# Eight plain scatter tables in place of one accumulating table, with 112 slots an expert

## The reference, cut to what matters

```python
scores = sigmoid(x @ w_router)                 # 512 tokens x 64 experts
top_idx = the 8 best of scores + bias, from the 4 best of 8 groups
w = scores[top_idx] / sum * 2.5
for expert e, for each of its tokens t:        # 4096 assignments in all
    g, u = split(x[t] @ w_exp_gu[e])           # 1024 -> 2 x 256
    routed[t] += w[t, e] * ((silu(g) * u) @ w_exp_down[e])   # 256 -> 1024
out = layer_norm(2**0.25 * x + routed + shared_expert(x))
```

## Time and profile before

| what | value |
|---|---|
| median of 3 runs | 3268.33 us (3266.63 to 3270.45) |
| the profiled execution | 3269.64 us, its span 3267.9 us |
| granted TensorE clock, mean | 0.938 |
| TensorE matmul busy | 2857.8 us (87%) |
| VectorE busy | 2117.2 us (65%) |
| ScalarE busy | 1468.9 us (45%) |
| POOL busy | 191.9 us (6%) |
| DMA, both queues | 437.13 MB, 32.4% and 8.2% of 16 engines |

### The profile page before, as it was taken

The page is one execution under the profiler, slowest core; times in us unless marked ns, Lnnn a source line. Parts: engine busy times, 40 slices in busy tenths (PEclk is TensorE's granted clock), DMA queues, the critical chain, the costliest instruction groups (busy, mean ns, idle before and its releaser), DMA issues.

```text
span 3267.9 us, 36369 instructions
## 1 busy us (share of the span) xinstructions
PE 2857.8 (87%) x12231; PEld 2118.2 (65%) x12231; DVE 2117.2 (65%) x3326; ACT 1468.9 (45%) x2215; POOL 191.9 (6%) x168
## 2 busy tenths in 40 slices
PE   8899899999989899999988888879776988988883
PEld 6777677887768578877663333655345877777772
DVE  4787546775298577753457885431326988888884
ACT  5666432223255432232224453331224877777772
POOL 0000000000000000000000000000001222222220
PEclk9999999999999899999998888989887999999996
DMA  3222223222311032233220000212018999999995
GB/s 105 59 64 63 79 78 103 86 94 71 104 61 61 26 98 82 77 89 85 83 77 23 0 1 26 78 64 78 30 69 292 356 361 361 361 361 361 361 361 160
DMA packets 292139, 437.13 MB, mean 134 GB/s; under 512 B 27371, under 2 KB 172195, under 8 KB 292035
## 3 DMA queue, kind: packets, MB, share of 16 engines
q1 hardware_dynamic: 272163, 363.42, 32.4%
q0 software_dynamic: 19872, 72.36, 8.2%
HBM read 394.84 MB, written 40.89 MB: 133 GB/s over the span
## 4 chain that ended last, share of the span: by engine, by line
PE 60%; SPq 18%; DVE 11%; ACT 4%; DMA 3%; issue 3%; DVEq 0%; POOLq 0%; ACTq 0%; PEldq 0%
PE tp L1001 36%; SPq L773 12%; SPq L780 5%; PE tp L960 5%; PE tp L1316 1%; PE tp L1054 1%; PE tp L1056 1%; PE tp L1055 1%; DMA uT<-in_w_exp_gu 1%; DMA ytab<-arena 1%; PE mp L1020 1%; PE mp L1034 1%; PE tp L1306 1%; DVE wring_r L2163 1%; PE mp L1231 1%
## 5 line engine op out<-in xcount | busy, mean ns | idle before, releaser
L1001 PE MATMUL tp<-sq_r,arena_r 128*128 128x512 f32 x1152 | 464.4, 403 | 43.2 <-DVE uT_r L2176 25.7
L1001 PE MATMUL tp<-sq_r,wring_r 128*128 128x512 f32 x1152 | 460.1, 399 | 0.0
L1001 PE MATMUL tp<-uT_r,arena_r 128*128 128x512 f32 x1152 | 457.7, 397 | 0.0
L1001 PEld LDWEIGHTS tp<-sq_r,arena_r 128*128 128x128 f32 x1152 | 218.7, 190 | 102.9 <-issue 48.4
L1001 PEld LDWEIGHTS tp<-uT_r,arena_r 128*128 128x128 f32 x1152 | 219.3, 190 | 54.6 <-issue 1.9
L1001 PEld LDWEIGHTS tp<-sq_r,wring_r 128*128 128x128 f32 x1152 | 218.8, 190 | 53.4
L1001 PE MATMUL tp<-arena_r,wring_r 128*128 128x512 f32 x608 | 242.5, 399 | 0.0
L2163 DVE TENSOR_TENSOR wring_r<-wring,arena_r 128x2048 fp32r<-128x2048 f32 x80 | 179.7, 2287 | 79.0 <-ACT arena_r L1581 79.0
L1581 ACT ACTIVATE arena_r<-wring 128x2048 fp32r<-128x2048 f32 x80 | 148.5, 1904 | 56.0 <-DMA wring<-in_w_in 21.5
L1001 PE MATMUL tp<-arena_r,sq_r 128*128 128x512 f32 x480 | 154.6, 404 | 19.6 <-DVE arena_r L2176 19.6
L1800 ACT ACTIVATE arena<-arena 128x512 f32<-128x512 f32 x44 | 27.9, 634 | 292.7 <-DVE arena L2244 292.6
(11 more groups left out here) (446 smaller groups left out, 6267.1 us busy)
## 6 DMA issues: line engine op xcount, KB each, us to landing
arena<-in_w_exp_down SPq DMA_DIRECT2D x64, 1024.0 KB, 18.2
wring<-in_w_exp_gu SPq DMA_DIRECT2D x64, 768.0 KB
uT<-in_w_exp_gu SPq DMA_DIRECT2D x32, 768.0 KB
sq<-in_w_exp_gu SPq DMA_DIRECT2D x32, 768.0 KB
wring<-in_f_up_w SPq DMA_DIRECT2D x22, 1024.0 KB, 5.2
wring<-in_f_up_w SPq DMA_DIRECT2D x44, 512.0 KB, 6.8
wring<-in_w_exp_gu SPq DMA_DIRECT2D x32, 512.0 KB
wring<-in_f_down_w SPq DMA_DIRECT2D x32, 448.0 KB, 5.6
```

What stands on the lines that cost most here:

```text
L1001: ins = nc.tensor.matmul(b[:], parts[wp][:, kk, m * P:(m + 1) * P], xparts[xp][:, kk, :], start=n_k == 0 and q == 0, stop=n_k == k - 1 and ...
```

## The change

Every token has eight experts, and its results are ranked by expert number. The kernel keeps, beside the token number, the rank of each assignment (`ranks`, a running count of the mask), and each expert writes its rows to row `rank * 512 + token` of an eight times longer `ytab`, by a plain indirect DMA. Residual and shared expert go to their own table `rest`. Empty slots get indices beyond the table, which the DMAs skip (`bounds_check`); `CAP` goes from 128 to 112. The scatter no longer waits for the one before, only for its buffer.

At the end the eight rank tables and `rest` are read into buffers as these come free, from the last three experts on; five of them are added on VectorE, three by TensorE with an identity matrix into PSUM. The norm is fused into two passes. Rank r of a token comes from expert 56 + r at the latest, so table r is complete early.

Beside this: the weights are laid with adjacent rows on one partition, and x and the activation are transposed with a stride to match; the transposes of the activation move behind those of the next x; several semaphores of the first block's scan go, and phase ends behind the expert loop move into the crowded branch.

```diff
-        NE, CAP, NTOK, RING = 64, P, T, 8
+        NE, CAP, NTOK, RING, TOPK = 64, 112, T, 8, 8
...
-        xtab = nc.dram_tensor("xtab", (NTOK + P, D), F32).ap()
-        ytab = nc.dram_tensor("ytab", (NTOK + P, D), F32).ap()
+        xtab = nc.dram_tensor("xtab", (NTOK, D), F32).ap()
+        rest = nc.dram_tensor("rest", (NTOK, D), F32).ap()
+        ytab = nc.dram_tensor("ytab", (TOPK * NTOK, D), F32).ap()
...
-                gu = pick(A["w_exp_gu_2"][0].rearrange("e (k p) n -> p e k n", p=P), e)
+                gu = pick(A["w_exp_gu_2"][0].rearrange("e (p k) n -> p e k n", p=P), e)
...
+                sp.wait_ge(moe["gu"], NE - 3)
+                all_added(NE - 8)
+                load_rank(0, first_ranks)
+                sp.wait_ge(moe["gu"], NE - 2)
+                all_added(NE - 7)
+                load_rank(1, first_ranks)
+                sp.wait_ge(moe["down"], NE - 3)
+                load_norm()
+                sp.wait_ge(moe["gu"], NE - 1)
+                all_added(NE - 6)
+                load_rank(2, first_ranks)
+                all_added(NE - 5)
+                load_rank(3, middle_ranks)
+                sp.wait_ge(moe["gu"], NE)
+                all_added(NE - 4)
+                load_rank(4, middle_ranks)
+                sp.wait_ge(moe["down"], NE - 1)
+                load_rest()
+                all_added(NE - 3)
+                load_rank(5, late_ranks)
+                all_added(NE - 2)
+                load_rank(6, late_ranks)
+                sp.wait_ge(moe["down"], NE)
+                all_added(NE - 1)
+                load_last_rank()
...
                 wait(moe["y"], n * 2 + 2)
-                wait(moe["scattered"], 16 * n)
...
-                G.indirect_dma_start(out=ytab, out_offset=bass.IndirectOffsetOnAxis(ap=sidx[q], axis=0), in_=ye[b],
-                                     in_offset=None, compute_op=ALU.add).then_inc(moe["scattered"], 16)
+                G.indirect_dma_start(out=ytab, out_offset=bass.IndirectOffsetOnAxis(ap=ridx[q][0:CAP, :], axis=0), in_=ye[b][0:CAP, :],
+                                     in_offset=None, bounds_check=TOPK * NTOK - 1, oob_is_err=False).then_inc(scattered[b], 16)
...
+                x = xe[b][0:CAP, :].rearrange("p (f k) -> p k f", k=NK)
                 for k in range(NK):
-                    ins = nc.tensor.transpose(tp[2 + k // 4][:, (k % 4) * P:(k % 4 + 1) * P], xe[b][:, k * P:(k + 1) * P], ident[:])
+                    ins = nc.tensor.transpose(tp[2 + k // 4][:, (k % 4) * P:(k % 4) * P + CAP], x[:, k, :], ident[0:CAP, 0:CAP])
...
+                if not fixed or e >= 1:
+                    m_actturn(e - 1)
                 m_gu(e, k % 2, k % 4)
                 if not fixed or e >= 1:
                     m_down(e - 1, (k + 1) % 2, (k - 1) % 4)
-                m_actturn(e)
...
+                V.tensor_scalar(sidf, mp[1][:, 4:5], slotcol[:, 1:2], slotcol[:, 0:1], ALU.mult, ALU.add)
+                ins = V.tensor_reduce(rsw[q], mp[1][:, 0:4].rearrange("p (a b) -> p a b", b=2), AX.X, ALU.add)
...
+                V.tensor_tensor(sidx[q], sidf, mp[1][:, 0:1], ALU.add)
+                V.tensor_tensor(ridx[q], sidf, rsw[q][:, 0:1], ALU.add).then_inc(moe["conv"], 1)
...
+            for c in range(TC):
+                for half in range(2):
+                    s = slice(512 * half, 512 * half + 512)
+                    for r in (5, 6):
+                        nc.tensor.matmul(total[c][half][:], ident[:], rank_rows[r][:, c, s], start=r == 5, stop=False)
+                pe.wait_ge(row_in[c], 16 * 2)
+                for half in range(2):
+                    s = slice(512 * half, 512 * half + 512)
+                    ins = nc.tensor.matmul(total[c][half][:], ident[:], rank_rows[7][:, c, s], start=False, stop=True)
+                ins.then_inc(rank_sums, 1)
...
+            dve.wait_ge(first_ranks, 16 * 5)
+            for r in (1, 2):
+                for c in range(TC):
+                    add_rows(c, rank_rows[r])
+            dve.wait_ge(middle_ranks, 16 * 3)
+            for rows in (rank_rows[3], rank_rows[4], rest_rows):
+                for c in range(TC):
+                    add_rows(c, rows)
...
-                link(V.tensor_scalar(fin[c], fin[c], mv[:, c, 0:1], rs3[:, c:c + 1], ALU.subtract, ALU.mult))
-                link(V.tensor_tensor(fin[c], fin[c], g3, ALU.mult))
-                V.tensor_tensor(fin[c], fin[c], b3, ALU.add).then_inc(fin_ready, 1)
+                link(V.scalar_tensor_tensor(fin[c], fin[c], mv[:, c, 0:1], g3, ALU.subtract, ALU.mult))
+                V.scalar_tensor_tensor(fin[c], fin[c], rs3[:, c:c + 1], b3, ALU.mult, ALU.add).then_inc(fin_ready, 1)
```

## The result

The changed kernel takes 3236.0 us (median of 4 runs, 3234.57 to 3240.29), against 3269.4 for the kernel before on the same chip: ratio 0.9905, 95% interval 0.9890 to 0.9921. So it is 33 us faster, not 90; the time lies above the predicted range of 3160 to 3225. The profiled execution took 3234.57 us, its span is 3232.8.

The account below looks back on a forecast made before the run. Transfers (11.63 us an expert) bound most of the loop, VectorE (10.04) its start. Forecast: 9.9 us steps save 91.0, the tail adds 2.4, a smaller first gather saves 1.0: -89.6, so 3179 us, range 3160 to 3225.

Parts of the forecast that it names:

- not 0.9: TensorE's strided transposes, a rival at 0.17: doubled load time adds 0.9 us an expert, step 10.6 us, total 3221.
- rival (c): Expert loop: POOL's indirect DMAs with limit checks become the bound; at 13 us a step, total 3365; chance 0.04.
- The crowded pass: Rival: an expert over 112 tokens reruns everything, over 2000 us; under 1%, 0.02 together with the unknown.
- the 621.2 of the sum: Expert loop: 8.3 + 10.4, then 60 steps of 9.9, last 8.5 us; 621.2 against 712.2, 91.0 less.
- Transfers per expert: Expert loop's DMA time: plain scatter and 112 slots with skips bring transfers from 11.63 to about 9.6 us an expert.
- Both cases there: Transfers an expert: 9.1 us if skips are free and rows even; 10.05 if full slots load some engines or skips cost full.
- 8.26 us for the weights: Expert loop: weight transfers per engine and expert, read from the kernel before and kept unchanged in the forecast.
- a share of 1.05: Expert loop: DMA engines' share in the kernel before, by which the summed transfer times were divided.
- Whether it saves anything the rows do not price, and I take zero: Expert weights: adjacent rows give longer runs and cannot cost more packets; saving taken as zero.
- Rival (b): Expert loop: transfers stay the bound through a dear scatter or slowed engines; 11.1 us a step, 3251; chance 0.07.
- The tail: After the last silu: VectorE's additions and chunks, no waits for tables; 59.0 us against 56.6, 2.4 more.
- Most is read while the last three experts compute, since the weights are all in by then: Tail tables, 18.9 MB: tables 0 to 4 and rest in 11 us after last silu, last by 27.

Follow-up runs that it names:

- e1: Changed kernel with expert weight rows apart again and transposes reading without a stride; 3235.25 us, 0.9898 of the kernel before.
- e4: Changed kernel with weight rows apart, unstrided transposes and filled slots dealt evenly over sixteen blocks of seven partitions; 3187.77 us, 0.9750 of the kernel before.
- e3: Changed kernel with slot numbers dealt so filled slots lie evenly in sixteen blocks of seven partitions; 0.9769 of the kernel before, three executions of 3189 to 3195 us.
- e16: Changed kernel with 112 slots, gather and scatter DMAs of 128 rows, empty slots using spare rows, none skipped; 3199.03 us, 0.9792 of the kernel before.
- e15: Changed kernel with 112 slots, DMAs of 128 rows, nothing skipped and weight rows apart; 3219.78 us, 0.9846 of the kernel before.
- e12: Changed kernel with 112 slots, but gather and scatter name 128 rows, the last 16 always skipped; 3212.82 us, 0.9833 of the kernel before.
- e6: Changed kernel without the skip: empty slots read and write spare rows, DMAs of 112 rows; 3247.81 us, 0.9930 of the kernel before.
- e5: Changed kernel with the first 56 slots filling every other block of seven partitions, the rest between; 3241.92 us, 0.9923 of the kernel before.
- e13: Changed kernel with 104 slots in place of 112; 3246.63 us, 0.9938 of the kernel before.
- e14: Changed kernel with 120 slots in place of 112; 3260.98 us, 0.9978 of the kernel before.
- e7: e4 without reading the tables of ranks 1 to 6, all additions made from the table of the rest; 3181.43 us, 0.9732 of the kernel before.
- e2: Changed kernel with each gate/up DMA taking every third row, runs of 2 KB at 16 KB pitch; 3246.74 us, 0.9944 of the kernel before.
- e17: e12 with its slot numbers dealt in turn over fourteen blocks of eight partitions; 3215.39 us, 0.9848 of the kernel before.

## Why the prediction was wrong

*The direction and the engines' steps were right.* Compute was forecast at 9.82 to 9.9 us a step. It is 9.83 in e1's early phase, 9.93 all through e4, and 10.0 with the strided transposes in the change's early phase and all through e3; the stride costs 0.07 to 0.17 and not 0.9. POOL never bound; its scatter takes 1.3 us. But rival (c)'s "the descriptors skipped are not built" does not hold: the trace has a packet of 4 bytes for each skipped slot. (The change's q0 has 10803 packets in 84 DMAs from 2650 to 3100 us, 128.6 each, against 112 rows and 16 more small ones.) The crowded pass did not run. Where transfers stopped binding (e3, e4, e16) the loop spans 625.0, 619.7 and 620.5 us against the 621.2 of the sum.

*The step that failed* is in "Transfers per expert": "I take transfers at about 9.6, between the first two". Both cases there keep 8.26 us for the weights and a share of 1.05, and price only gather and scatter anew. But both numbers had been read beside 128-row DMAs that skip nothing, and neither was a constant. By the rows above a step of the change carries 3.146 MB x 45.4 / 16 = 8.93 us of weights and 0.145 x 10.7 = 1.55 us of gather and scatter, 10.48 us, over a share of 0.98: 10.7. The term for gather and scatter was well sized (1.31 to 2.29); the weights were 0.67 us dearer and the share 1.05 was not reached. Either miss alone would have been hidden behind compute: 10.48 / 1.05 is 9.98, and (8.26 + 1.55) / 0.98 is 10.01. "Whether it saves anything the rows do not price, and I take zero" was wrong too: e15 against e16 is 0.6 us an engine and expert, to be had only with DMAs of 128 rows. Rival (b) had "skips slow the engines" at a chance of 0.07, but its 11.1 came from a dear scatter, which is not there.

The runs put two causes in the place of that step, and a third one in part:
- 112 rows a DMA in place of 128: 23 us (the change against e12, filled slots first in both), 49 us without the skip (e6 against e16). Shown. Why the weights' packets grow dearer by it (42.7 against 38.7 engine-us per MB without the skip) is open.
- Filled slots first, so that some engines are full and some nearly empty: 45 to 47 us with 112 rows (the change against e3, e1 against e4). Shown: with the rows evenly spread the loop is the forecast's. With e3, too, 112 rows are no handicap that shows, since compute binds there.
- The skip, where the filled rows are uneven. With 112 rows it gains 12 us all the same (the change against e6), and 57 when they are even (e3 against e6). With 128 rows and the filled slots first it loses 14 us (e12 against e16): it takes gather and scatter from 0.262 x 9.92 = 2.60 to 0.139 x 10.17 = 1.41 us a step, and the weights go from 38.7 to 42.6 engine-us per MB, 7.61 to 8.38 us; of 1.19 saved 0.77 comes back, the share falls from 1.02 to 0.97, and the step ends 0.25 longer (0.07 of that is there in the early phase already, 10.0 against 9.93, where no transfer binds). e16 differs from e12 in two things, since without the skip all engines should carry the same; whether skipped slots or uneven engines make the weights dear is open.

The price per MB is no full account either: e3's packets are dearer than e12's in both queues (42.9 and 45.1 against 42.6 and 42.2), and e3 is 22 us faster.

The Trainium skill ("DMA: Bandwidth & Descriptors", "Why a DMA increments its semaphore by 16 and not by 1") gives the number of engines as the largest up to 16 that divides the rows: 16 for 112 and 128, 13 for 104, 15 for 120. e5 agrees with sevens, and e13 and e14, slower than the change by 11 and 25 us, agree with fewer engines; but the rule puts both 112 and 128 on 16 engines, where the runs show 23 to 49 us between them. The Trainium skill ("SBUF — State Buffer", "Door 1: The DMA port swizzle") would have each strided element pay for a 16-byte line; the measured 15% on eight loads together at a step of 32 bytes is small, and a step of 8 bytes, two elements to a line, is not free: two loads take 0.32 us in place of 0.20.

*The tail* was forecast at 59.0 us and took 77.1. VectorE's own work was sized a little high: 54.2 us where the sum has 59.0 (the twenty additions take 22.8 and not 25.0, a chunk 5.92 and not 6.2). What came on top are 22.9 us of waits for tables, where the forecast had none. The step that failed: "Most is read while the last three experts compute, since the weights are all in by then". That held before, when the share was 0.17 between the last two silus. The 19.9 MB need 48 to 58 us at 345 to 410 GB/s wherever they stand, and they queue behind weights that are themselves late: from 3130 to 3159 us the share was 0.90. The rate of 5 us for 2 MB is near what was reached (367 GB/s from 3159 to 3196), and the start of the queue was wrong. e7 supports this only in part, since it keeps 7 us of waiting without six of the tables.

Where the 90 us went: 34.0 in the loop (655.2 against 621.2), 18.1 in the tail (77.1 against 59.0) and 2.3 at the first silu (+1.3 against -1.0), 54.4 together; 89.6 less 54.4 is 35.2, the difference of the spans to 0.1.

The fastest version is e4, 3187.8 us (0.9750 of the kernel before, 0.985 of the change), with the 112-row DMAs and evenly dealt slots; e16 has the faster transfers but, in its profiled execution, came 10 us later to its loop and has 71.2 us of tail.

## What to carry to other kernels

Price a change of one stream of transfers by what it does to the others too: compute engine-us per MB for each queue before and after, because a share near 1 hides whether the engines move 345 or 419 GB/s. If an indirect DMA skips rows, spread the filled ones evenly over the engines, and check in the packets in flight that the spreading worked: that made the fastest kernels here, with 112 rows. If the filled rows stay first, give the DMA all 128 rows, even if sixteen carry nothing, and try moving empty rows to spare ones in place of skipping them. Drop an accumulating scatter first and alone: it was worth 79 us by itself. And a table read at the end costs its bytes over the full rate, counted from when the last weights are in by the new schedule, not by the old one.

## What the runs showed of the hardware that I had not expected

- The same bytes of weights cost from 38.7 (e16) to 47.1 engine-us per MB (e14), depending on the other queue's DMAs and on the runs in memory; runs of 2 KB at a pitch of 16 KB (e2) add 10 us to the kernel.
- Sixteen skipped rows more make a kernel 23 us faster (e12), where the filled rows come first.
- In the trace's packets, the 56 filled rows of one gather early in the loop take 2.08 us with at most 10 in flight when they stand first, and 1.13 us with 18 in flight when they are dealt out over blocks of seven (e3). Dealt over blocks of eight, in DMAs of 128 rows, they take 2.2 us with 10 in flight (e17), as if they stood first: the two row counts are dealt to the engines by different patterns. Which ones, the runs don't show.
- One execution of e3 (10749 us) and one of the kernel before (15201 us) were several times as long as the others. I have no explanation for either.
